# Hybrid decoder layer in two-part fp32: low-part products last, and the modulation matrices one slot later in SP's queue

## The chip, the core and the metric

The kernel runs on one core of one Trainium2 chip. The engines of the core are PE (TensorE, with PEld for its weight loads), DVE (VectorE), ACT (ScalarE), POOL (GpSimd) and SP (SyncE, which here issues all the transfers). The metric is the device time of one execution in microseconds. The time of the kernel before is the median of three runs.

## What is computed

One decoder layer on 512 tokens with model width 1024, then a final RMSNorm. Cut to what matters:

```python
mod = silu(c) @ w_ada + b_ada                        # 6 x 1024 columns
sh1, sc1, gt1, sh2, sc2, gt2 = split(mod, 6)
h = rms_norm(x, g_norm_mix) * (1 + sc1) + sh1
hq, hf, hi, hg, aq, ak, av, ga, gb = split(h @ w_in)  # 8704 columns
y_a = hgrn2_mix(hq, hf, hi, hg, lower_bounds)        # gated linear recurrence, 4 heads
y_b = dilated_mixture(aq, ak, av)                    # 3 groups of 4 heads
merged = sigmoid(ga) * (y_a @ w_branch_a) + sigmoid(gb) * (y_b @ w_branch_b)
x = x + (1 + gt1) * (merged @ w_out)
h2 = rms_norm(x, g_norm_ffn) * (1 + sc2) + sh2
u_gate, u_val = split(h2 @ w_up)
x = x + (1 + gt2) * ((gelu(causal_dwconv(u_gate)) * u_val) @ w_down)
return rms_norm(x, g_final)
```

## The kernel before

**Two-part products.** Every large product is made of three passes. A weight tile and an activation tile are each split into a high part (rounded to fp32r) and a low part (the rest). For each slice k of 128 rows PE multiplies high by high, high weights by low activations, and low weights by high activations, all into one PSUM bank (`three_passes`, products recorded at line L934). A product of 128 x 512 elements is the usual one.

**Units.** The weights come in 75 units of 1 MB. Units 0 to 33 are 256 columns of `w_in`, 34 and 35 are `w_branch_a`, 36 and 37 `w_branch_b`, 38 to 41 `w_out`, 42 to 63 `w_up`, 64 to 74 `w_down`. For each unit:

- SP loads it into `w_raw` (`load_unit`, L465), after it has waited at L463 until the unit two before has both its high and its low part, since it shares the buffer;
- ACT copies it to `w_hi` (L659, `unit_high`), when it has landed and PE has finished the last tile of the unit two before;
- POOL subtracts to give `w_lo` (L590, four instructions, `low_part`);
- PE does `products(u)`: it waits for the low part (`lo_done`), then fills two output tiles (48 products), or four: of 256 columns in units 4, 5, 8, 11, 38 to 41, and over four slices k only in units 34 to 37. A tile takes one of the three banks 0 to 2 in turn. `claim` waits until the bank's tile before has been read out, `filled` tells ACT and DVE that the tile is there. Before the change a tile gets all its products and then the next tile starts.

**Slots.** All engines run the same loop `for u in range(U_UP)`. PE does `products(u)` and then `small(u)`: the small products of the recurrence and the attention, which are laid out over the slots. DVE and ACT do `small_results(u)` and then `evacuate(u)`, each in its own order.

**Modulation.** The modulation matrices 0 to 7 are dealt with at the start. Matrices 8 to 23 (1 MB each, `w_ada`, two buffers `ada2`) are spread over slots 17 to 27 by `MOD_UNITS`: one in slots 17, 18, 21, 24, 25 and 27, two in slots 19, 20, 22, 23 and 26. In slot u DVE scales and adds the matrix (`partial_sums`, L1284 to L1291, the result in `part2`, counted by `part_done`), before it reads out the tiles of unit u. PE ends `small(u)` with eight (or four) products of one column on these sums, after it has waited for `part_done`. SP issues the transfer (L506) when the buffer is free, that is when DVE has summed the matrix two before. SP is strictly in order, so whatever stands behind that wait goes out later.

**Units 36 and 37.** For each of the four tiles DVE multiplies (L1604) and adds (L1606), ACT rounds to `m_hi` (L864), and DVE subtracts to `m_lo` (L1608), before it turns to the next tile. ACT's copy of the high part of unit 38 stands behind the fourth `m_hi` of unit 36.

Of the kernel before, what the change touches and what calls it, by code (L numbers as in the profile page):

```python
# [29 lines left out]
P = 128  # L30
D = 1024
S = 512
KT = D // P
TT = S // P
HEADS = 4
# [21 lines left out]
U_A = U_GB + 4  # L57
U_B = U_A + 2
U_OUT = U_B + 2
# [21 lines left out]
MOD_SLOT, MOD_TWICE = 17, (19, 20, 22, 23, 26)  # L81
MOD_UNITS = {}
# [63 lines left out]
def tiles_of(u):  # L146

    if U_PAIR <= u < U_HG:
        p, what = divmod(u - U_PAIR, 3)
        return 4 if what == 2 and pair(p)[2] == 1 else 2  # L150
    if U_HI <= u < U_PAIR or U_A <= u < U_UP:
        return 4
    return 2
# [41 lines left out]
BANKS = plan_banks()  # L195
# [17 lines left out]
def layer_kernel(nc, x, c, w_ada, b_ada, g_norm_mix, w_in, lb_logits, g_hg_norm, w_branch_a, w_branch_b, w_out,  # L213
                 g_norm_ffn, w_up, conv_w, conv_b, w_down, g_final, out):
    with ExitStack() as ctx:
# [7 lines left out]
        whi = [at(f"w_hi{i}", 136 + 8 * i, [P, 2048], F32R) for i in range(2)]  # L223
        wlo = [at(f"w_lo{i}", 152 + 8 * i, [P, 2048], F32R) for i in range(2)]
# [4 lines left out]
        h_hi = at("h_hi", 168, [P, KT, S], F32R)  # L229
        h_lo = at("h_lo", 184, [P, KT, S], F32R)  # L230
# [24 lines left out]
        ya_hi = at("ya_hi", 40, [P, HEADS, S], F32R)  # L255
        ya_lo = at("ya_lo", 48, [P, HEADS, S], F32R)
# [12 lines left out]
        yb_hi = at("yb_hi", 64, [P, HEADS, S], F32R)  # L269
        yb_lo = at("yb_lo", 76, [P, HEADS, S], F32R)  # L270
# [67 lines left out]
        bank = [ctx.enter_context(nc.psum_tensor(f"bank{i}", [P, 512], F32)) for i in range(8)]  # L338
# [8 lines left out]
        hi_done = sem("hi_done")  # L347
        share_in = [sem(f"share_in{j}") for j in range(KT // 2)]
        hi_share, lo_share = sem("hi_share"), sem("lo_share")
        lo_done = sem("lo_done")  # L350
# [36 lines left out]
        ybfull_done, ybhi_done, yblo_done = sem("ybfull_done"), sem("ybhi_done"), sem("yblo_done")  # L387
# [9 lines left out]
        def claim(eng, name):  # L397

            b, n = BANKS[name]
            if n:  # L400
                eng.wait_ge(free[b], n)
            return bank[b]

        def filled(ins, name):
            ins.then_inc(full[BANKS[name][0]], 1)
# [50 lines left out]
        def _(sp):  # L456
# [34 lines left out]
            for u in range(U_UP):  # L491
                if u == U_B + 2:

                    ready(sp, ("g", U_B - 1, 3))
                    sp.wait_ge(yblo_done, HEADS)
                    sp.dma_start(x1[:, :, :], x_tok).then_inc(x_again, 16)

                    sp.dma_start(gf_row[:, :], g_final.rearrange("(a d) -> a d", a=1).broadcast_to([P, D])).then_inc(gf_in, 16)
                if u >= 3:
                    load_unit(u, unit_source(u), u % 2)  # L500
                if u == MOD_SLOT:
                    ready(sp, ("o", HEADS - 1))
                for n in MOD_UNITS.get(u, ()):
                    if n >= MOD_FIRST + 2:
                        sp.wait_ge(part_done, n - 1)
                    sp.dma_start(ada2[n % 2][:, :, :], cols_of(w_ada, 256 * n)).then_inc(ada2_in[n % 2], 16)  # L506
# [425 lines left out]
        def _(pe):  # L932
            def mm(o, lhsT, rhs, start=True, stop=True, **kw):
                return pe.matmul(o, lhsT, rhs, start=start, stop=stop, **kw)  # L934
# [30 lines left out]
            def unit_parts(u, slot, width):  # L965
                pe.wait_ge(lo_done, u + 1)
                return [w[slot][:, :].rearrange("p (k c) -> p k c", c=width) for w in (whi, wlo)]
# [22 lines left out]
            def plain_tokens(t):  # L990
                return lambda a: a[:, t * P:(t + 1) * P]

            def products(u):
                hT = (h_hi, h_lo)
                n = tiles_of(u)
                width = 512 if U_A <= u < U_OUT else 256
                parts = unit_parts(u, 2 if u == 2 else u % 2, width)
                for t in range(n):
                    b = claim(pe, ("g", u, t))
                    if u == U_A and t == 0:  # L1000
                        pe.wait_ge(yalo_done, HEADS)
                    if u == U_B and t == 0:
                        pe.wait_ge(yblo_done, HEADS)
                    if u >= U_OUT:
                        merged = (m_hi, m_lo)
                        if u == U_OUT and t == 0:

                            token_tile(b[:, 0:256], parts, merged, plain_tokens(0), range(KT - 1))
                            b1 = claim(pe, ("g", u, 1))
                            token_tile(b1[:, 0:256], parts, merged, plain_tokens(1), range(KT - 1))  # L1010
                        kts = range(KT - 1, KT) if u == U_OUT and t < 2 else range(KT)
                        ins = token_tile(b[:, 0:256], parts, merged, plain_tokens(t), kts)
                    elif u >= U_A:
                        ins = feature_tile(b[:, :], parts, t * P, (ya_hi, ya_lo) if u < U_B else (yb_hi, yb_lo), HEADS)
                    elif n == 4:
                        ins = token_tile(b[:, 0:256], parts, hT, plain_tokens(t))
                    else:
                        ins = feature_tile(b[:, :], parts, t * P, hT)
                    filled(ins, ("g", u, t))
# [696 lines left out]
```

## Time and profile before

| | |
|---|---|
| three runs | 1008.28, 1010.56, 1012.77 us; median 1010.56 |
| profiled execution, its own time | 1011.39 us |
| its span | 1009.7 us |
| mean granted clock of TensorE | 0.982 |
| PE busy | 954.7 us, 95% of the span, 4911 products |
| PEld busy | 812.8 us, 80% |
| DVE, POOL, ACT busy | 466.9, 463.4, 367.9 us |

The profiled time is 1.69 us more than its span: that much lies outside the first and the last instruction. A product of PE is recorded with its latency, and the next starts before it has ended, so one reads a stage of PE from start to start: 48 products in 11.03 us, for instance. The granted clock is 1.00 at 2.4 GHz and 0.50 at 1.2 GHz; a stretch in between is a mixture in time of the two.

### The profile page before, as it was taken

How to read it: one execution, taken by the hardware profiler on the slowest of the kernel's cores; microseconds unless marked ns; L12 is line 12 of the kernel's file. 1: busy time of each engine (PE TensorE's matmuls, PEld its weight loads, DVE VectorE, ACT ScalarE, POOL GpSimd, SP SyncE). 2: the span in 40 equal slices, each digit the busy share in tenths (PEclk: the TensorE clock that was granted, in tenths of full speed). 3: DMA queues.
4: the chain of work that ended last, by engine and by line, in shares of the span. 5: the costliest groups of instructions: out<-in, count | busy, mean ns of one | idle time of the engine just before them, and what ended most of it. 6: DMA issues, size and time to landing. Idle time of an engine off the chain costs nothing.

```text
span 1009.7 us, 12653 instructions
## 1 busy us (share of the span) xinstructions
PE 954.7 (95%) x4911; PEld 812.8 (80%) x4911; DVE 466.9 (46%) x720; ACT 367.9 (36%) x499; POOL 463.4 (46%) x382
## 2 busy tenths in 40 slices
PE   2699999999999989899999999899999999999995
PEld 2578989998888878788778899688888888888884
DVE  5855366665337858886642554622222322200006
ACT  6443332424234141444222334544435544412113
POOL 3669542534123243534455455553543453453544
PEclk9989999999999989999999999999999999999998
DMA  9722222121151756362222533123223223223212
GB/s 322 223 83 84 84 84 84 43 84 43 43 167 43 242 175 217 117 209 84 83 84 84 188 101 109 42 83 122 86 83 125 83 83 109 100 87 122 84 42 83
DMA packets 94817, 111.33 MB, mean 110 GB/s; under 512 B 1930, under 2 KB 88118, under 8 KB 94774
## 3 DMA queue, kind: packets, MB, share of 16 engines
q1 hardware_dynamic: 94774, 110.72, 33.3%
q8 instruction: 31, 0.51, 0.2%
q14 instruction: 12, 0.10, 0.0%
HBM read 108.62 MB, written 2.10 MB: 110 GB/s over the span
## 4 chain that ended last, share of the span: by engine, by line
PE 43%; issue 31%; POOL 18%; DVE 5%; ACT 1%; DMA 1%; SPq 0%; POOLq 0%; ACTq 0%; DVEq 0%
PE bank L934 43%; POOL w_lo L590 17%; DVE x L1686 1%; DVE part L1284 1%; DMA x_in<-in_x_dram 1%; DVE h_lo L1301 1%; DVE gelu L1685 0%; DVE part L1295 0%; DVE ada L1284 0%; DVE part L1286 0%; DVE ada L1286 0%; ACT w_hi L659 0%; DVE part L1291 0%; POOL rstd L551 0%; ACT xn_in L703 0%
## 5 line engine op out<-in xcount | busy, mean ns | idle before, releaser
L590 POOL TENSOR_TENSOR w_lo<-w_raw,w_hi 128x512 fp32r<-128x512 f32 x292 | 395.8, 1386 | 494.1 <-ACT w_hi L659 494.1
L934 PE MATMUL bank<-h_hi,w_hi 128*128 128x512 f32 x832 | 332.8, 400 | 9.1 <-POOL w_lo L590 6.0
L934 PE MATMUL bank<-h_hi,w_lo 128*128 128x512 f32 x832 | 329.1, 396 | 0.0
L934 PE MATMUL bank<-h_lo,w_hi 128*128 128x512 f32 x832 | 328.7, 395 | 0.0
L659 ACT ACTIVATE w_hi<-w_raw 128x2048 fp32r<-128x2048 f32 x73 | 139.4, 1909 | 238.1 <-PE bank L934 180.8
L934 PEld LDWEIGHTS bank<-h_hi,w_hi 128*128 128x128 f32 x832 | 159.8, 192 | 44.4 <-POOL w_lo L590 6.2
L934 PEld LDWEIGHTS bank<-h_hi,w_lo 128*128 128x128 f32 x832 | 159.0, 191 | 33.9
L934 PEld LDWEIGHTS bank<-h_lo,w_hi 128*128 128x128 f32 x832 | 159.7, 192 | 32.9
L934 PE MATMUL bank<-w_lo,act_hi 128*128 128x512 f32 x176 | 68.5, 389 | 0.0
L934 PE MATMUL bank<-w_hi,act_lo 128*128 128x512 f32 x176 | 68.5, 389 | 0.0
L934 PE MATMUL bank<-w_hi,act_hi 128*128 128x512 f32 x176 | 68.5, 389 | 0.0
L1660 DVE SCALAR_TENSOR_TENSOR conv<-bank,convc,conv 128x511 f32<-128x511 f32 x22 | 16.4, 745 | 107.8 <-ACT conv L898 107.8
L1685 DVE TENSOR_TENSOR gelu<-bank,g_row 128x512 f32<-128x512 f32 x8 | 5.5, 682 | 107.9 <-PE bank L934 107.9
L1284 DVE SCALAR_TENSOR_TENSOR part<-ada,csilu,part 128x256 f32<-128x256 f32 x64 | 43.8, 685 | 0.0
L1670 DVE TENSOR_TENSOR gelu<-gelu,bank 128x512 f32<-128x512 f32 x22 | 15.1, 687 | 58.3 <-PE bank L934 45.2
L898 ACT ACT_TABLE_LOAD x11 | 14.1, 1283 | 73.8 <-PE bank L934 73.8
L934 PEld LDWEIGHTS bank<-w_hi,act_hi 128*128 128x128 f32 x176 | 33.0, 188 | 6.9
L934 PEld LDWEIGHTS bank<-w_hi,act_lo 128*128 128x128 f32 x176 | 33.0, 188 | 6.9
L934 PEld LDWEIGHTS bank<-w_lo,act_hi 128*128 128x128 f32 x176 | 33.0, 188 | 6.7
L1284 DVE SCALAR_TENSOR_TENSOR ada<-ada,csilu 128x256 f32<-128x256 f32 x56 | 37.4, 669 | 0.0
L934 PE MATMUL bank<-w_hi,m_hi 128*128 128x256 f32 x128 | 36.3, 284 | 0.3 <-POOL w_lo L590 0.3
L934 PE MATMUL bank<-w_hi,h_hi 128*128 128x256 f32 x128 | 36.5, 285 | 0.0
(247 smaller groups left out, 1329.2 us busy)
## 6 DMA issues: line engine op xcount, KB each, us to landing
w_raw<-in_w_in_dram SPq DMA_DIRECT2D x32, 1024.0 KB, 5.2
ada<-in_w_ada_dram SPq DMA_DIRECT2D x24, 1024.0 KB, 7.2
w_raw<-in_w_up_dram SPq DMA_DIRECT2D x22, 1024.0 KB, 5.1
w_raw<-in_w_down_dram SPq DMA_DIRECT2D x11, 1024.0 KB, 4.8
w_raw<-in_w_out_dram SPq DMA_DIRECT2D x4, 1024.0 KB, 6.5
x_in<-in_x_dram SPq DMA_DIRECT2D x4, 512.0 KB, 7.1
w_raw<-in_w_in_dram SPq DMA_DIRECT2D x8, 256.0 KB, 8.5
w_raw<-in_w_branch_a_dram SPq DMA_DIRECT2D x2, 1024.0 KB, 4.9
```

Of the source, the lines that this page charges most:

```text
L590: ins = pool.tensor_tensor(wlo[slot][:, cols], raw[slot][:, cols], whi[slot][:, cols].bitcast(F32), ALU.subtract)
L659: act.activation(whi[bufs][:, :], raw[bufs][:, :], ACT.Copy).then_inc(hi_done, 1)
L898: act.activation(conv[:, t, :], bank[t][:, :], ACT.Identity, scale=CW[:, bass.ds(2 * i + (2 * FT + t), 1)], bias=CW[:, bass.ds(2 * i + (3 ...
L934: return pe.matmul(o, lhsT, rhs, start=start, stop=stop, **kw)
L1284: ins = stt(dst, unit[:, k, :], sc, dst, ALU.mult, ALU.add)
L1301: tt(h_lo[:, k, :], h_part(which, k), h_hi[:, k, :].bitcast(F32), ALU.subtract).then_inc(h_lo_done[k % 2], 1)
L1660: stt(tt_, bank[t][:, 0:S - 1], CW[:, bass.ds(2 * i + (FT + t), 1)], tt_, ALU.mult, ALU.add).then_inc(tap_done, 1)
L1670: tt(gelu[:, t, :], gelu[:, t, :], bank[bk][:, :], ALU.mult).then_inc(free[bk], 1)
L1685: link(tt(gelu[:, half, :], b[:, :], g2_row[:, cols], ALU.mult))
L1686: tt(x1[:, t, cols], x1[:, t, cols], gelu[:, half, :], ALU.add).then_inc(x2_done, 1)
```

## The change

First, PE. For the units 2 to 37 the first two output tiles are now made together: tile 0 gets all its products with the high part of the weights, then tile 1 gets all of its own, then PE waits for the low part, and then both get the products with it. Before the first of them PE waits only for the high part (`hi_done`). Tiles 2 and 3, where a unit has them, are made as before. The number and the form of the products are the same. The bank of tile 1 is claimed 8 products earlier than before (4 in units 34 to 37), and tile 0 is finished 16 products later (8 in units 34 to 37). Second, SP. The modulation matrices of slot u are issued behind the weights of unit u+1, where they stood behind those of unit u.

```diff
@@ SP's queue
                 if u >= 3:
                     load_unit(u, unit_source(u), u % 2)
-                if u == MOD_SLOT:
+                if u - 1 == MOD_SLOT:
                     ready(sp, ("o", HEADS - 1))
-                for n in MOD_UNITS.get(u, ()):
+                for n in MOD_UNITS.get(u - 1, ()):
                     if n >= MOD_FIRST + 2:
                         sp.wait_ge(part_done, n - 1)
                     sp.dma_start(ada2[n % 2][:, :, :], cols_of(w_ada, 256 * n)).then_inc(ada2_in[n % 2], 16)
@@ PE
+            def first_two_tiles(u, width):
...
+                pe.wait_ge(hi_done, u + 1)
+                if u == U_A:
+                    pe.wait_ge(yalo_done, HEADS)
+                if u == U_B:
+                    pe.wait_ge(yblo_done, HEADS)
...
+                for t in range(2):
+                    claim(pe, ("g", u, t))
+                    for k in range(kts):
+                        one_pass(t, k, hi, a_hi, k == 0, False)
+                        one_pass(t, k, hi, a_lo, False, False)
+                pe.wait_ge(lo_done, u + 1)
+                for t in range(2):
+                    for k in range(kts):
+                        ins = one_pass(t, k, lo, a_hi, False, k == kts - 1)
+                    filled(ins, ("g", u, t))
+
             def products(u):
...
+                if u < U_OUT:
+                    first_two_tiles(u, width)
+                    if n == 2:
+                        return
                 parts = unit_parts(u, 2 if u == 2 else u % 2, width)
                 for t in range(n):
+                    if u < U_OUT and t < 2:
+                        continue
                     b = claim(pe, ("g", u, t))
-                    if u == U_A and t == 0:
-                        pe.wait_ge(yalo_done, HEADS)
-                    if u == U_B and t == 0:
-                        pe.wait_ge(yblo_done, HEADS)
```

PE in unit 36 before the change, where tile 0 (bank2) ends and tile 1 (bank0) begins. `yb_hi` and `yb_lo` are the parts of the activations, `w_hi0` and `w_lo0` those of the weights.

```order
L934 MATMUL bank2<-yb_hi_102,w_hi0_51 128x512
L934 MATMUL bank2<-yb_lo_103,w_hi0_51 128x512
L934 MATMUL bank2<-yb_hi_102,w_lo0_53 128x512
L934 MATMUL bank0<-yb_hi_102,w_hi0_51 128x512
L934 MATMUL bank0<-yb_lo_103,w_hi0_51 128x512
L934 MATMUL bank0<-yb_hi_102,w_lo0_53 128x512
```

PE in unit 36 after the change, from the end of tile 1's high products to the start of tile 2 (bank1).

```order
L934 MATMUL bank0<-yb_hi_102,w_hi0_51 128x512
L934 MATMUL bank0<-yb_lo_103,w_hi0_51 128x512
L934 MATMUL bank2<-yb_hi_102,w_lo0_53 128x512 x4
L934 MATMUL bank0<-yb_hi_102,w_lo0_53 128x512 x4
L934 MATMUL bank1<-yb_hi_102,w_hi0_51 128x512
L934 MATMUL bank1<-yb_lo_103,w_hi0_51 128x512
L934 MATMUL bank1<-yb_hi_102,w_lo0_53 128x512
```

Tile 0 was finished as the 12th product of the unit, before tile 1 began; now it is finished as the 20th, and tile 1 as the 24th, as before.

SP's queue before the change, from the weights of unit 19 to those of unit 21 (L465 the weights, L506 the modulation matrices).

```order
L465 DMA w_raw1_50<-in_w_in_dram 128x8x256
L506 DMA ada2_0_123<-in_w_ada_dram 128x8x256
L506 DMA ada2_1_124<-in_w_ada_dram 128x8x256
L465 DMA w_raw0_49<-in_w_in_dram 128x8x256
L506 DMA ada2_0_123<-in_w_ada_dram 128x8x256
L506 DMA ada2_1_124<-in_w_ada_dram 128x8x256
L465 DMA w_raw1_50<-in_w_in_dram 128x8x256
```

SP's queue after the change, again from the weights of unit 19 to those of unit 21.

```order
L465 DMA w_raw1_50<-in_w_in_dram 128x8x256
L506 DMA ada2_1_124<-in_w_ada_dram 128x8x256
L465 DMA w_raw0_49<-in_w_in_dram 128x8x256
L506 DMA ada2_0_123<-in_w_ada_dram 128x8x256
L506 DMA ada2_1_124<-in_w_ada_dram 128x8x256
L465 DMA w_raw1_50<-in_w_in_dram 128x8x256
```

The weights of unit 21 stood behind matrices 12 and 13 of slot 20; now they stand behind matrices 10 and 11 of slot 19 and ahead of those two.

## Rows read from the trace of the kernel before

**Rows 1.** The page: issues of the modulation matrices, their size, median us to landing.

```profile
ada<-in_w_ada_dram SPq DMA_DIRECT2D x24, 1024.0 KB, 7.2
```

**Rows 2.** Waits of PE: total us, times, longest us.

```profile
PE bank L934 <- POOL w_lo L590: 6.3, 4, 3.1
PE bank L934 <- DVE wg_lo L1529: 1.6, 1, 1.6
```

**Rows 3.** Stretches: length; busy (count) of PE, PEld, DVE, ACT, POOL; clock; DMA; GB/s.

```profile
344.13:355.16 11.03, 11.03 (x51) 9.10 (x50) 8.87 (x22) 1.15 (x1) 0.00 (x0) 1.00 1.01 322
361.02:374.56 13.54, 13.54 (x48) 10.89 (x49) 7.90 (x11) 4.42 (x18) 5.61 (x4) 0.80 0.33 109
406.72:419.34 12.62, 12.62 (x49) 10.24 (x50) 9.88 (x17) 5.74 (x19) 5.11 (x4) 0.86 0.47 154
486.08:498.71 12.63, 12.63 (x50) 10.02 (x49) 4.87 (x5) 1.23 (x2) 5.19 (x4) 0.87 0.24 83
641.50:860.00 218.50, 218.50 (x965) 180.91 (x965) 59.63 (x86) 102.98 (x104) 99.22 (x80) 1.00 0.29 96
```

**Rows 4.** Timeline (start, us, ...) of PE at the starts of units 21, 23, 24.

```profile
356.94 0.95 PE L934 MATMUL bank<-ones,part 128*128 128x1 f32 x8
361.02 0.79 PE L934 MATMUL bank<-h_hi,w_hi 128*128 128x512 f32 x1 [3.13 <-POOL w_lo L590]
...
389.48 1.00 PE L934 MATMUL bank<-ones,part 128*128 128x1 f32 x8
390.34 0.48 PE L934 MATMUL bank<-h_hi,w_hi 128*128 128x512 f32 x1
...
403.11 0.95 PE L934 MATMUL bank<-ones,part 128*128 128x1 f32 x8
406.72 0.50 PE L934 MATMUL bank<-h_hi,w_hi 128*128 128x512 f32 x1 [2.65 <-POOL w_lo L590]
```

**Rows 5.** Timeline of SP: matrices 12 and 13, weights of unit 21, matrices 15 and 16.

```profile
336.12 7.77 SPq L506 DMA_DIRECT2D ada<-in_w_ada_dram  x2
344.01 0.51 SPq L465 DMA_DIRECT2D w_raw<-in_w_in_dram  x1
...
354.40 15.06 SPq L506 DMA_DIRECT2D ada<-in_w_ada_dram  x2
```

**Rows 6.** Timeline of ACT and POOL: the two parts of unit 21's weights.

```profile
354.01 1.92 ACT L659 ACTIVATE w_hi<-w_raw 128x2048 fp32r<-128x2048 f32 x1 [15.96 <-DMA w_raw<-in_w_in_dram]
...
356.01 4.96 POOL L590 TENSOR_TENSOR w_lo<-w_raw,w_hi 128x512 fp32r<-128x512 f32 x4 [12.79 <-ACT w_hi L659]
```

**Rows 7.** Timeline of DVE: matrices 13 and 15 begin, 16 ends, then unit 22's tiles.

```profile
350.85 0.35 DVE L1286 TENSOR_SCALAR part<-ada,csilu 128x256 f32<-128x256 f32 x1 [1.76 <-DMA ada<-in_w_ada_dram]
...
378.73 0.34 DVE L1286 TENSOR_SCALAR part<-ada,csilu 128x256 f32<-128x256 f32 x1
...
389.39 0.43 DVE L1291 TENSOR_TENSOR part<-part,ada 128x256 f32<-128x256 f32 x1
389.73 1.28 DVE L1566 COPY ka<-bank 128x512 f32<-128x512 f32 x2
```

**Rows 8.** Timeline of DVE in units 36 and 37, without most of its rows.

```profile
563.08 0.69 DVE L1604 TENSOR_TENSOR sgb<-sgb,bank 128x512 f32<-128x512 f32 x1 [2.94 <-PE bank L934]
...
566.16 0.68 DVE L1604 TENSOR_TENSOR sgb<-sgb,bank 128x512 f32<-128x512 f32 x1
...
569.26 0.68 DVE L1604 TENSOR_TENSOR sgb<-sgb,bank 128x512 f32<-128x512 f32 x1
...
571.97 0.68 DVE L1604 TENSOR_TENSOR sgb<-sgb,bank 128x512 f32<-128x512 f32 x1
```

**Rows 9.** Timeline of ACT, POOL and PE: the weights of unit 38 and its start.

```profile
573.94 1.90 ACT L659 ACTIVATE w_hi<-w_raw 128x2048 fp32r<-128x2048 f32 x1
...
575.92 6.41 POOL L590 TENSOR_TENSOR w_lo<-w_raw,w_hi 128x512 fp32r<-128x512 f32 x4 [8.53 <-ACT w_hi L659]
...
582.39 0.38 PE L934 MATMUL bank<-w_hi,m_hi 128*128 128x256 f32 x1 [0.31 <-POOL w_lo L590]
```

More of the change, by code:

```diff
@@ L991, in plain_tokens, with one_pass @@
                 return lambda a: a[:, t * P:(t + 1) * P]
+            def first_two_tiles(u, width):
+                slot = 2 if u == 2 else u % 2
+                hi, lo = (w[slot][:, :].rearrange("p (k c) -> p k c", c=width) for w in (whi, wlo))
+                tokens_out = tiles_of(u) == 4 and u < U_A
+                a_hi, a_lo = (h_hi, h_lo) if u < U_A else (ya_hi, ya_lo) if u < U_B else (yb_hi, yb_lo)
+                kts = KT if u < U_A else HEADS
+                pe.wait_ge(hi_done, u + 1)
[3 more added lines that the diff above has]
+                    pe.wait_ge(yblo_done, HEADS)
+                def one_pass(t, k, w, a, start, stop):
+                    tile, o = slice(t * P, (t + 1) * P), bank[BANKS["g", u, t][0]]
+                    if tokens_out:
+                        return mm(o[:, 0:256], a[:, k, tile], w[:, k, :], start, stop, skip_group_check=True)
+                    return mm(o[:, :], w[:, k, tile], a[:, k, :], start, stop, skip_group_check=True)
+                for t in range(2):
[8 more added lines that the diff above has]
+                    filled(ins, ("g", u, t))
             def products(u):
```

## The prediction, made before the changed kernel ran

> **What bounds the kernel now.** PE is busy in 95% of the span of 1009.7 us, so the question is only where PE stands still and where its clock is low. I read first the waits of PE. In the part that the change touches (units 2 to 37) two releasers matter: the low part of the weights, 6.3 us in four waits of which the longest is 3.1, and once the DVE chain that makes the merge weights, 1.6 us [rows 2]. The timeline puts 3.13 and 2.65 us of them at the starts of units 21 and 24 [rows 4] and 0.31 us at unit 38 [rows 9]; the 0.2 us left of the 6.3 stand at unit 27. Then I read stretches for the clock. A unit of 48 products takes 11.03 us at clock 1.00, that is 0.230 us for a product; unit 21 took 13.54 us at 0.80, unit 24 took 12.62 us at 0.86, and unit 30, right behind the wait for the merge weights, 12.63 us at 0.87 [rows 3]. Each slow unit is one that begins after PE stood still: after 3.13, 2.65 and 1.57 us [rows 2, 4]. Behind the 0.31 us of unit 38 the clock stayed.
>
> Last I followed the low part of unit 21 back. POOL made it from 356.01 to 360.97, ACT the high part from 354.01 to 355.93, and ACT had waited 15.96 us for the transfer [rows 6]. SP issued that transfer at 344.01, right behind two modulation matrices, of which the second went out only at 336.12 + 7.77 = 343.89, when DVE had freed its buffer [rows 5]. So the stall is one of SP's order: weights queue behind a modulation matrix that queues behind DVE. Unit 24 is the same case.
>
> **The change part by part.**
>
> *The number of products* does not change, nor their form, so PE's own work costs nothing more. The order of the banks changes from product to product at most as it does in the loop of the gate projections, which alternates two banks after every three products and ran at clock 1.00 over 218.50 us with 965 recorded products, 0.226 us each [rows 3].
>
> *The waits for the low part.* After eight one-column products PE needs 0.86 us to the first product of the next unit where nothing holds it (389.48 to 390.34) [rows 4]. So unit 21 could have begun at 356.94 + 0.86 = 357.80 and began at 361.02: 3.22 us. Unit 24: 403.97 against 406.72, 2.75 us. Unit 27: the 0.2 us left above. Sum 6.17 us. Either half of the change takes them away alone. With the split, unit 21 needs only the high part, there at 355.93, before 357.80; the low part is needed 32 products later, 32 x 0.230 = 7.4 us, and it was there 3.2 us after 357.80. With SP's new order the weights of unit 21 stand behind matrices 10 and 11, whose place in DVE is a slot earlier; they go out before the pair that now stands at 336.12 to 343.89 [rows 5], at least 7.9 us earlier than at 344.01, so the high part too is there before 357.80 with time to spare, and the low part, 7.0 us behind its start (354.01 to 360.97), by 353.1. What is late next at these starts is nothing: PE itself.
>
> *The clock.* Unit 21 took 13.54 - 11.03 = 2.51 us more than a unit at full clock, unit 24 took 12.62 - 11.03 = 1.59 us more [rows 3]. The idle time that stood before both is gone, so I count both: 4.10 us.
>
> *The modulation matrices one slot later.* Each is issued when both the weights ahead of it are out and DVE has summed the matrix two before. The first condition is new by one unit. In the trace the second is the later one except for matrices 15 and 20, one each behind the low part of a unit that came late. Matrix 15 was issued at 354.40 [rows 5] and would now wait for the low part of unit 21, which ended at 360.97 when its weights were late [rows 6]. Even then, with 7.2 us for the transfer [rows 1], it would have landed at 368.2, and DVE came to it at 378.73 [rows 7]. Cost 0. The second matrix of a double slot lands as late as now: DVE waited 1.76 us for matrix 13 [rows 7], and a load of weights followed it at once (343.89 and 344.01 [rows 5]), as one does in the new order.
>
> *DVE and PE at the end of the double slots.* These are tight. The sum of matrix 16 ends at 389.82, PE's one-column products on it began at 389.48 and took 1.00 instead of 0.95 us [rows 4, 7]. DVE starts its slot when PE ends the one before, so the pair moves together and the stall does not grow. Bound: 0 to 0.5 us in each of slots 19, 22, 26; I take 0, as the row shows it.
>
> *Tile 0 later, bank of tile 1 earlier.* In a unit of 48 products tile 0 is there 16 x 0.230 = 3.7 us later, and PE wants its bank again at the 16th product of the next unit. The latest reading is in unit 22: DVE frees tile 0 halfway through 389.73 to 391.01, at about 390.4 [rows 7]; PE claims that bank 16 products into unit 23, at 390.34 + 3.7 = 394.0 [rows 4]. Margin 3.6 us. It costs nothing there or elsewhere in this stage, but 3.6 us is all the cover there is.
>
> *Units 36 and 37* have no such cover. There DVE and ACT take as long for a tile as PE: 3.08 us for the first (563.08 to 566.16, while POOL works), 2.71 us for the third (569.26 to 571.97) [rows 8], against 12 x 0.230 = 2.76 us of PE. DVE was idle for 2.94 us ahead of the first tile, waiting for PE. That tile now comes 8 x 0.230 = 1.84 us later, and nothing behind it can catch up except the 3.08 - 2.71 = 0.37 us that the first step may win if POOL's work lies less on it. So the fourth `m_hi`, and ACT's copy of unit 38's weights behind it at 573.94, come 1.47 to 1.84 us later, and so does POOL's low part, 575.92 to 582.33, for which PE already waits 0.31 us [rows 9]. Unit 38 is not split. Loss 1.5 to 1.8 us; I take 1.6. The idle time becomes 0.31 + 1.6 = 1.9 us. Behind 1.57 us of idle time the clock fell in unit 30, where some small products stood between, and it cost 12.63 - 11.03 = 1.60 us [rows 3]; behind 0.31 it did not. Bounds 0 and 1.6 us; I take 0 and keep the other end for the range.
>
> Here the Trainium skill has a rule on the cause of the 3.08 us: "SBUF — State Buffer", section "SBUF: two separate sides", says that a DVE operation with two SBUF inputs and a GpSimd operation shut each other out of a port pair. By it the 0.37 us comes back only if POOL's low part of unit 37 ends before DVE's first addition, so the loss would be the upper end, 1.8 us.
>
> *The wait for the merge weights*, 1.57 us [rows 2], ends a DVE chain that starts when PE ends slot 27, so it moves with PE and stays, and its lost clock with it.
>
> **Sum.** 6.17 + 4.10 - 1.6 = 8.67 us. On the profiled execution's own time 1011.39 - 8.67 = 1002.7. That execution lay 0.83 us over the median of the runs, 1010.56, so as a median 1002.7 - 0.8 = **1001.9 us**.
>
> **The rivals.**
>
> *The cover in DVE is too thin (a wait takes the place of the one removed).* With PE no longer stalled, DVE and ACT have no slack from it. For it: the 0.05 us at 389.48 above. Price: 1 us in each of slots 19, 22 and 26, and one low-clock unit of 1.6 us: 4.6 us given back, 1001.9 + 4.6 = 1006.5. Nearly the same time comes if the idle time goes and the clock is lost elsewhere all the same: 1001.9 + 4.1 = 1006.0.
>
> *The loss at unit 38 doesn't come*, because the chain of DVE and ACT catches up in unit 36: 1001.9 - 1.6 = 1000.3; if unit 30 keeps its clock as well, another 1.6 less, 998.7.
>
> *Slower.* SP now waits for unit u+1's buffer (L463) before it may issue the matrices of slot u. If POOL's low part of unit u-1 ended later than DVE's sum of the matrix two before, and by more than the matrix lies in wait, DVE would stand for the transfer, PE behind its sums, and POOL behind PE. It decides from the point where the issue comes less than 7.2 us [rows 1] before DVE's use. In three double slots this is 3 x 7.2 = 21.6 us and, as in unit 21, 2.5 us of clock each: 29.1 us, which makes 1001.9 + 29.1 = 1031.0. Against it speaks the margin of matrix 15, 378.7 - 368.2 = 10.5 us.
>
> *Banks in turn.* Between two passes PE goes back to a bank that it left. The gate projections do so oftener, at clock 1.00 [rows 3]; were the clock lost for 1.6 us in each of the 36 units, the time would be 1001.9 + 57.6 = 1059.5. The Trainium skill, "TensorE: Matmul & The Clock Gate", section "A second HAM failure mode: psum-queue depth-cycling", reports a kernel in which cycling through banks made TensorE idle briefly and its clock swing. This case's 218.50 us at clock 1.00 does not agree with it.
>
> *The change does nothing* if something other than the weights holds PE at these starts: 1010.6.
>
> **Chances.** Forecast (1000.3 to 1003.6) 0.61; thin cover or clock lost elsewhere (1003.6 to 1007) 0.19; no loss at unit 38 (998.5 to 1000.3) 0.11; nothing 0.04; slower 0.04; banks 0.01. About 0.5%, 5 us, is what a measurement of this kernel can tell from no change; the bound lies at 1005.5. Of the second case I put a third below it. Faster by over 0.5%: 0.61 + 0.11 + 0.06 = 0.78. Within: 0.13 + 0.04 = 0.17. Slower: 0.05. Range for 8 in 10: down to 999.0, and up to 1006.5 for most of the second case, with the 1.6 us of clock at unit 38 inside it.
>
> **What would show it.** Right: no idle time of PE at the starts of units 21 and 24, both at about 11.1 us; the transfer of unit 21's weights issued before 336 us on the old scale; the wait of PE at unit 38 near 1.9 us, with `m_hi` and ACT's copy of unit 38 late by the same; the wait for the merge weights as before. Wrong: waits of PE on DVE's `part` or on a bank's release in slots 18 to 28, a DVE wait for `ada` much over 1.76 us, or units 36 and 37 ending without a longer wait behind them.

## The result, and the profile after

The changed kernel takes **1004.07 us** (median of 8 runs, 1002.87 to 1007.33) where the kernel before, on the same chip, took 1010.35 us (8 runs, 1006.61 to 1013.98). The ratio is 0.9946, 95% interval 0.9925 to 0.9968: about 0.5% faster. The medians lie 6.3 us apart; the ratio is estimated from all runs, here and below, and isn't the quotient of the two medians. The profiled execution took 1005.12 us with a span of 1003.4 us, against 1011.39 and 1009.7 before. The forecast was 1001.9, its range 999.0 to 1006.5.

The waits of PE (total us, times, longest us), after:

```profile
PE bank L934 <- POOL w_lo L590: 2.1, 1, 2.1
PE bank L934 <- DVE wg_lo L1561: 1.6, 1, 1.6
...
PE bank L934 <- DVE part L1323: 0.8, 1, 0.8
```

The four waits for `w_lo`, 6.3 us in all [rows 2], are now one of 2.1 us. The wait for the merge weights, `wg_lo`, stayed at 1.6. A wait for `part` is new in this profile.

The timeline of PE at the starts of units 21 and 24, after (start, us, ...):

```profile
357.69 0.49 PE L934 MATMUL bank<-h_hi,w_hi 128*128 128x512 f32 x1
...
398.07 0.49 PE L934 MATMUL bank<-h_hi,w_hi 128*128 128x512 f32 x1
```

Neither start has a wait in brackets any more, against 3.13 and 2.65 us [rows 4]. Unit 21 starts 3.33 us earlier than before, unit 24 8.65 us earlier.

SP's timeline around the weights of unit 21 (line 465) and the matrices (line 506), after:

```profile
327.34 0.37 SPq L506 DMA_DIRECT2D ada<-in_w_ada_dram  x1
327.81 0.53 SPq L465 DMA_DIRECT2D w_raw<-in_w_in_dram  x1
```

The weights of unit 21 went out at 327.81; before the change they went out at 344.01, behind a matrix that had to wait for its buffer [rows 5].

Stretches, after (length; busy and count of PE, PEld, DVE, ACT, POOL; clock; DMA; GB/s):

```profile
357.69:368.72 11.03, 11.03 (x51) 9.05 (x50) 7.67 (x22) 3.91 (x17) 4.64 (x4) 1.00 0.58 183
398.07:409.10 11.03, 11.03 (x51) 9.05 (x50) 8.62 (x24) 5.19 (x18) 4.63 (x4) 1.00 0.88 279
475.35:482.18 6.83, 6.83 (x17) 4.91 (x16) 5.40 (x6) 0.91 (x2) 5.91 (x4) 0.50 0.07 25
477.17:490.60 13.43, 13.43 (x50) 10.64 (x49) 4.02 (x4) 1.23 (x2) 4.45 (x3) 0.81 0.24 78
```

Units 21 and 24 take 11.03 us each at clock 1.00, against 13.54 at 0.80 and 12.62 at 0.86 [rows 3]. Unit 30 got worse: 13.43 us at 0.81 against 12.63 at 0.87 [rows 3]. The 0.50 in the third row is the lower level, 1.2 GHz, and it lasts 6.83 us.

The end of slot 26, after: timelines of POOL, DVE and PE.

```profile
427.08 5.46 POOL L590 TENSOR_TENSOR w_lo<-w_raw,w_hi 128x512 fp32r<-128x512 f32 x4 [7.86 <-ACT w_hi L659]
...
431.31 1.51 DVE L1316 SCALAR_TENSOR_TENSOR part<-ada,csilu,part 128x256 f32<-128x256 f32 x1
432.74 0.47 DVE L1316 SCALAR_TENSOR_TENSOR ada<-ada,csilu 128x256 f32<-128x256 f32 x1
...
437.54 0.43 DVE L1323 TENSOR_TENSOR part<-part,ada 128x256 f32<-128x256 f32 x1
...
438.02 0.61 PE L934 MATMUL bank<-ones,part 128*128 128x1 f32 x4 [0.81 <-DVE part L1323]
438.49 0.48 PE L934 MATMUL bank<-h_hi,w_hi 128*128 128x512 f32 x1
```

As long as POOL works on the low part of unit 27, DVE's multiply-add takes 1.51 us, and after that 0.47. Four of DVE's operations are stretched in this way (three multiply-adds, and the scaling before them from 0.35 to 1.46 us), about 4 us in all, and the sum of the second matrix ends at 437.97, when PE already waits for it. In the kernel before, POOL made this low part from 442.14, over the last three operations of the chain, and PE lost only the 0.20 us for `w_lo`:

```profile
442.56 1.51 DVE L1284 SCALAR_TENSOR_TENSOR part<-ada,csilu,part 128x256 f32<-128x256 f32 x1
...
442.14 5.89 POOL L590 TENSOR_TENSOR w_lo<-w_raw,w_hi 128x512 fp32r<-128x512 f32 x4 [12.69 <-ACT w_hi L659]
...
448.09 0.51 PE L934 MATMUL bank<-h_hi,w_hi 128*128 128x512 f32 x1 [0.20 <-POOL w_lo L590]
```

Last, the start of unit 38, after: timelines of DVE (first tile of unit 36), ACT, POOL and PE.

```profile
556.78 0.69 DVE L1636 TENSOR_TENSOR sgb<-sgb,bank 128x512 f32<-128x512 f32 x1 [4.75 <-PE bank L934]
557.50 1.42 DVE L1638 TENSOR_TENSOR sgb<-sgb,sga 128x512 f32<-128x512 f32 x1
...
567.15 0.63 ACT L864 ACTIVATE m_hi<-sgb 128x512 fp32r<-128x512 f32 x1 [2.08 <-DVE sgb L1638]
567.69 1.90 ACT L659 ACTIVATE w_hi<-w_raw 128x2048 fp32r<-128x2048 f32 x1
...
569.67 6.38 POOL L590 TENSOR_TENSOR w_lo<-w_raw,w_hi 128x512 fp32r<-128x512 f32 x4 [11.30 <-ACT w_hi L659]
...
576.10 0.39 PE L934 MATMUL bank<-w_hi,m_hi 128*128 128x256 f32 x1 [2.13 <-POOL w_lo L590]
```

DVE waits 4.75 us for the first tile instead of 2.94 [rows 8], and PE waits 2.13 us at unit 38 instead of 0.31 [rows 9]: 1.81 and 1.82 us more.

**The account of the span**, by start times (before minus after, rows above and [rows 3, 4, 9]):

| point | before | after | earlier by | step |
|---|---|---|---|---|
| unit 21 starts | 361.02 | 357.69 | 3.33 | |
| unit 24 ends | 419.34 | 409.10 | 10.24 | |
| unit 27 starts | 448.09 | 438.49 | 9.60 | -0.64 |
| unit 30 starts | 486.08 | 477.17 | 8.91 | -0.69 |
| unit 30 ends | 498.71 | 490.60 | 8.11 | -0.80 |
| unit 38 starts | 582.39 | 576.10 | 6.29 | -1.82 |
| span ends | 1009.7 | 1003.4 | 6.3 | 0 |

### The profile page after: what moved, and what is told of

Same layout as the page of the kernel before. It is cut to its first block, busy times and chain, and to the rows that moved or that the text cites. A ratio compares the mean times of both kernels' runs of the same rounds, so it can differ in the third digit from the quotient of the medians.

```text
span 1003.4 us, 12661 instructions
## 1 busy us (share of the span) xinstructions
PE 950.4 (95%) x4911; PEld 809.4 (81%) x4911; DVE 465.7 (46%) x720; ACT 368.3 (37%) x499; POOL 460.5 (46%) x382
## 4 chain that ended last, share of the span: by engine, by line
PE 43%; issue 30%; POOL 18%; DVE 5%; ACT 1%; DMA 1%; SPq 0%; POOLq 0%; ACTq 0%; DVEq 0%
PE bank L934 43%; POOL w_lo L590 17%; DVE x L1718 1%; DVE part L1316 1%; DMA x_in<-in_x_dram 1%; DVE h_lo L1333 1%; DVE gelu L1717 0%; DVE part L1327 0%; DVE ada L1316 0%; DVE part L1318 0%; DVE ada L1318 0%; ACT w_hi L659 0%; DVE part L1323 0%; POOL rstd L551 0%; ACT xn_in L703 0%
## 5 line engine op out<-in xcount | busy, mean ns | idle before, releaser
L934 PE MATMUL bank<-h_hi,w_lo 128*128 128x512 f32 x832 | 257.8, 392 | 0.0
L934 PE MATMUL bank<-w_lo,m_hi 128*128 128x256 f32 x128 | 36.2, 283 | 0.0
L934 PE MATMUL bank<-w_hi,m_lo 128*128 128x256 f32 x128 | 36.2, 283 | 0.0
```

## The experiments

The theory to test: SP's order alone removes the stalls; the split has nothing left to cover after it, and in units 36 and 37 it costs 1.8 us. Its rivals: the split carries part of the gain, or the loss at unit 38 has another cause. Three groups of kernels ran, each with the kernel before beside it. Medians are compared only within a group, ratios also between groups. Medians in us, ratio to before:

| kernel | before | median (range) | ratio, 95% |
|---|---|---|---|
| SP's order alone | 1006.72 | 1001.55 (998.42 to 1004.63) | 0.9947, 0.9921 to 0.9972 |
| split alone | 1006.72 | 1004.11 (1001.20 to 1006.36) | 0.9970, 0.9945 to 0.9995 |
| whole, 36 and 37 not split | 1006.72 | 1001.77 (998.46 to 1003.62) | 0.9951, 0.9923 to 0.9979 |
| before, unit 36 alone split | 1006.72 | 1011.60 (1003.25 to 1016.12) | 1.0038, 1.0007 to 1.0070 |
| whole change again | 1008.46 | 1004.10 (1001.60 to 1006.73) | 0.9961, 0.9943 to 0.9978 |
| whole, ACT copies early | 1008.46 | 1003.05 (1002.22 to 1005.12) | 0.9947, 0.9926 to 0.9968 |
| whole, merge weights later | 1008.46 | 1000.75 (999.75 to 1002.02) | 0.9923, 0.9899 to 0.9946 |
| SP's order, early copies, merge later | 1008.46 | 1000.83 (997.78 to 1001.50) | 0.9915, 0.9893 to 0.9937 |
| whole, `m_lo` one tile late | 1008.12 | 1001.25 (999.65 to 1005.49) | 0.9950, 0.9927 to 0.9973 |
| SP's order, merge later, `m_lo` late | 1008.12 | 997.96 (996.49 to 998.43) | 0.9905, 0.9878 to 0.9932 |
| whole, merge later, `m_lo` late | 1008.12 | 999.16 (998.07 to 1000.79) | 0.9919, 0.9892 to 0.9946 |
| kernel before again | 1008.12 | 1008.86 (1006.20 to 1011.21) | 1.0022, 0.9998 to 1.0045 |

### The whole change again

> The whole change once more, beside the others. My theory: as before, 0.9946 of the kernel before, PE waiting 2.1 us at unit 38. With the half of SP alone at 0.9947 and the half of PE alone at 0.997, it should not be faster than SP's half: about 1.8 us slower than that (1003 where SP's half gave 1001.6). Rival (the halves add up): 2.6 us faster than SP's half alone.

The ratio, 0.9961, overlaps the first one, and the gains of the two halves don't add up. This profile differs from the first at two places. Two stretches, unit 30 and unit 38:

```profile
476.55:487.64 11.09, 11.09 (x50) 8.93 (x49) 4.96 (x5) 1.23 (x2) 5.28 (x4) 1.00 0.29 95
...
573.14:586.25 13.11, 13.11 (x96) 13.11 (x97) 6.82 (x11) 4.60 (x9) 5.42 (x4) 0.87 0.30 90
```

Unit 30 kept its clock behind the same wait of 1.6 us, and unit 38 lost it behind its 2.1 us. In the first profile it was the other way round: unit 30 took 13.43 us at 0.81, and unit 38 ran at clock 1.00. So what a wait of this size costs in clock is not fixed by the program.

### SP's order alone

```
-                if u == MOD_SLOT:
+                if u - 1 == MOD_SLOT:
...
-                for n in MOD_UNITS.get(u, ()):
+                for n in MOD_UNITS.get(u - 1, ()):
```

> Only SP's new order, PE as before the change. My theory: the stalls at units 21 and 24 come from the order in SP's queue alone, so this half alone takes away 3.2 and 2.8 us of idle time and 4.1 us of low clock, as the whole change does, and it has not the loss of 1.8 us at unit 38, which is the split's: about 1.8 us faster than the whole change, 1002.3 as a median against 1004.1. PE at unit 38 waits 0.3 us as before. Rival (the split is what saves the starts): stalls stay, over 1008.

One of PE's waits, and the start of unit 38:

```profile
PE bank L934 <- DVE part L1291: 0.8, 1, 0.8
...
572.43 0.38 PE L934 MATMUL bank<-w_hi,m_hi 128*128 128x256 f32 x1 [0.31 <-POOL w_lo L590]
```

No stall is left at units 21, 24 and 27, unit 38 waits only 0.31 us, and the median is 5.2 us under that of before. The wait for `part` in slot 26 comes without any split: the weights of unit 27 are there earlier, so POOL starts earlier and stretches more of DVE's sums. The 1.8 us by which this kernel should beat the whole change show in the traces, as the missing loss at unit 38, but not in the times: the ratios are 0.9947 here and 0.9946 and 0.9961 for the whole change.

### The split alone

`first_two_tiles` for all units below `U_OUT`, SP's loop as before.

> Only PE's split, SP's order as before the change. My theory: the high part of unit 21 is there at 355.9, before PE wants it, so the starts of units 21 and 24 are as short as in the whole change, with the full clock, and unit 38 waits 2.1 us: about the time of the whole change, 1004.1. Rival (PE then waits in the middle of units 21 and 24 for the low part, or DVE's late reading of tile 0 shows): waits of 1 us and more inside these units, 1006 to 1009.

The start of unit 21 on PE, its low part on POOL, the start of unit 38 on PE:

```profile
356.12 0.49 PE L934 MATMUL bank<-h_hi,w_hi 128*128 128x512 f32 x1
...
352.15 5.00 POOL L590 TENSOR_TENSOR w_lo<-w_raw,w_hi 128x512 fp32r<-128x512 f32 x4 [10.17 <-ACT w_hi L659]
...
572.78 0.39 PE L934 MATMUL bank<-w_hi,m_hi 128*128 128x256 f32 x1 [2.13 <-POOL w_lo L590]
```

The split does what it says: PE starts at 356.12, though the low part is ready only at 352.15 + 5.00 = 357.15, and the unit runs through. But unit 38 again waits 2.13 us, now without SP's new order. This half alone gains 2.6 us in the median, half of the 5.2 us of SP's order; the 1.8 us at unit 38 are the larger part of the difference.

### The whole change, with units 36 and 37 left as they were

```
-                if u < U_OUT:
+                split = u < U_B
+                if split:
                     first_two_tiles(u, width)
```

> The whole change, but units 36 and 37 made tile by tile as before the change. My theory: the loss at unit 38 goes, PE waits 0.3 us there instead of 2.1, and the time is 1.8 us below that of the whole change, 1002.3. Rival (unit 38 is late because of SP's order or of the shift in time): the wait of 2.1 us stays, 1004.1.

```profile
574.39 0.39 PE L934 MATMUL bank<-w_hi,m_hi 128*128 128x256 f32 x1 [0.31 <-POOL w_lo L590]
```

PE's timeline at unit 38: the wait is back at 0.31 us. The median, 1001.77, is that of SP's order alone, 1001.55. The other 34 split units add nothing to SP's order that can be measured.

### The kernel before, with unit 36 alone split

`split = u == U_B`, SP's loop as before.

> The kernel before with the split in unit 36 alone. My theory: the first tile of unit 36 comes 1.8 us later, the chain of DVE and ACT can't catch up, ACT's copy of unit 38's weights and POOL's low part come 1.8 us later, and PE's wait at unit 38 grows from 0.3 to 2.1 us; stretches ahead of unit 36 as before; 1.8 us slower than before, 1012.2 against 1010.35. Rival: no change.

Start and stretch of unit 38:

```profile
583.67 0.39 PE L934 MATMUL bank<-w_hi,m_hi 128*128 128x256 f32 x1 [2.13 <-POOL w_lo L590]
...
583.67:596.77 13.10, 13.10 (x96) 13.10 (x97) 6.82 (x11) 4.60 (x9) 5.42 (x4) 0.87 0.29 91
```

One split unit suffices for the whole 2.13 us, so it is the late first tile of unit 36 that costs, as the prediction had it. In this profile the clock fell too: the 96 products took 13.10 us at 0.87, where the first profile of the whole change shows 11.61 at 1.00. The kernel is slower than before, 1.0038 with an interval above 1. The medians differ by 4.9 us, more than the 1.8 expected; the interval of the ratio, 0.7 to 7.0 us, includes the 1.8 and doesn't tell what the rest is.

### The whole change, ACT copying the high parts of units 38 and 39 ahead of `m_hi`

```
+                        if t == 3:
+                            unit_high(u + 2)
...
-                if u >= 2:
+                if u >= 2 and u not in (U_B + 1, U_B + 2):
                     unit_high(u + 1)
```

> The whole change, and ACT copies the high parts of units 38 and 39 ahead of the fourth m_hi of units 36 and 37 instead of behind it. My theory: the loss at unit 38 comes through ACT's order only, so POOL's low part of unit 38 is there before PE needs it, PE's wait falls from 2.1 us to below 0.5, and the time is 1.8 us below the whole change. Rival (PE then waits for m_lo, since DVE's chain is late by the same 1.8 us): the wait moves into unit 38, with m_lo as its releaser, and over 1 us of the 1.8 stays.

ACT, then PE in unit 38:

```profile
562.11 1.92 ACT L659 ACTIVATE w_hi<-w_raw 128x2048 fp32r<-128x2048 f32 x1
...
570.71 0.28 PE L936 MATMUL bank<-w_hi,m_hi 128*128 128x256 f32 x1
...
575.21 0.38 PE L936 MATMUL bank<-w_hi,m_hi 128*128 128x256 f32 x1 [2.09 <-DVE m_lo L1642]
```

ACT's copy of unit 38's weights is the first row. Unit 38 starts without a wait, and PE then waits 2.09 us inside it for `m_lo`. The wait has moved, not gone, as the rival said. The median is 1.05 us below that of the whole change in the same group, 1003.05 against 1004.10, which these runs can't tell from no change. The weights are one of two things that come late by the same time; the chain of DVE and ACT over the tiles, at 2.7 us a tile, is the other.

### The whole change, merge weights used one slot later

`SLOT_BC = SLOT_STAT + 4` instead of `+ 3`.

> The whole change, and the products that spread the merge weights (bc) stand one slot later, in slots 30 to 33. My theory: the wait of 1.6 us for the merge weights goes, and with it the low clock in unit 30 (0.8 to 2.5 us by its place): 2.4 to 4 us faster than the whole change. Rival (clock falls there for the small products, not for the wait): 1.6 us faster, and unit 30 or 31 still over 12 us.

```profile
473.46:484.43 10.97, 10.97 (x49) 8.82 (x47) 1.69 (x1) 3.00 (x3) 5.03 (x4) 1.00 0.45 144
```

The stretch is unit 30: 10.97 us at clock 1.00, and the wait for `wg_lo` is gone. The median falls by 3.35 us against the whole change in the same group, within the 2.4 to 4 expected. 1.6 us of it are the wait. That the rest is clock is a reading and not shown: the two profiles of the whole change lost about 3 and 0 us of clock behind that wait.

### SP's order, early copies and later merge weights, no split

> SP's half alone, with the early copy for units 38 and 39 and the merge products a slot later. My theory: no split, so no loss at unit 38, and the 0.3 us there and the stall for the merge weights gone: 2.5 to 4 us below SP's half alone (1001.6), so 998 to 999, the fastest of these.

The stretch of unit 38, and its first product behind the wait in it:

```profile
568.65:583.75 15.10, 13.24 (x97) 13.03 (x96) 8.31 (x14) 5.22 (x10) 5.49 (x4) 0.89 0.41 138
...
572.82 0.39 PE L936 MATMUL bank<-w_hi,m_hi 128*128 128x256 f32 x1 [1.86 <-DVE m_lo L1610]
```

Here unit 38 had only 0.31 us to lose, and the early copy brought in 1.86 us of wait and a lower clock: the copy of 1.92 us stands ahead of an `m_hi` for which DVE and PE wait. The copy was in its right place. The expected 998 to 999 us, the fastest of these, was missed: the median is 1000.83, that of the whole change with later merge weights alone (1000.75), and the error was to take the early copy for free.

### The whole change, `m_lo` one tile later in units 36 and 37

```
-                        dve.wait_ge(mhi_done, f + 1)
-                        tt(m_lo[:, f, :], ...)
+                        for e in {0: (), 1: (f - 1,), 2: (f - 1,), 3: (f - 1, f)}[t]:
+                            dve.wait_ge(mhi_done, e + 1)
+                            tt(m_lo[:, e, :], ...)
```

> The whole change, and VectorE in units 36 and 37 makes the low half of tile f-1 (m_lo) only after the multiply and add of tile f, so that it no longer waits 0.7 us in each tile for ScalarE's m_hi. Theory (the wait in front of unit 38 comes from the chain of VectorE and ScalarE on m_hi and m_lo, 2.7 us a tile, not from the weights' load): the wait of TensorE before unit 38 falls from 2.1 to under 0.5 us, and the kernel is about 1.8 us faster than the whole change, ratio to before near 0.993 to 0.994. Rival (the late start of the chain by the doubled pair 36/37 alone sets it, and the 0.7 us are slack): the wait stays at 2 us or goes inside unit 38 as a wait for m_lo, and the time is that of the whole change, 0.995 to 0.996.

Waits of PE, DVE at the first tile of unit 37 (multiplication, then addition), POOL at unit 38's low part:

```profile
PE bank L934 <- DVE m_lo L1641: 1.3, 1, 1.3
...
568.82 0.69 DVE L1636 TENSOR_TENSOR sgb<-sgb,bank 128x512 f32<-128x512 f32 x1 [1.73 <-PE bank L934]
569.54 1.80 DVE L1638 TENSOR_TENSOR sgb<-sgb,sga 128x512 f32<-128x512 f32 x1
...
568.25 5.95 POOL L590 TENSOR_TENSOR w_lo<-w_raw,w_hi 128x512 fp32r<-128x512 f32 x4 [8.72 <-ACT w_hi L659]
```

The wait for the weights is gone, as the theory said, but 1.3 us come back inside unit 38, as a wait for `m_lo`. The theory's under 0.5 us was wrong, and the rival came nearer: it named such a wait, if a longer one, and the time of the whole change, 0.995 to 0.996, and the ratio is 0.9950. Two things make `m_lo` late in unit 37. DVE now waits 1.73 us for PE at the first tile of that unit, which the split delivers later, and POOL's low part of unit 38 lies over DVE's work, where an addition takes 1.80 instead of 0.69 us. The next two kernels tell which counts: without the split POOL lies over DVE's work on unit 37 as well (one `m_lo` takes 1.78 us there), and PE doesn't wait for `m_lo`; with the split the 1.3 us are back. So the late first tile of unit 37 is what makes PE wait here. No run splits unit 37 alone.

### SP's order, later merge weights and later `m_lo`, with and without the split

> The kernel before with SP's reorder alone, the merge weights' statistics one slot later for their reader (SLOT_BC + 1), and the same delayed m_lo in units 36 and 37; no unit is split. Theory (with the weights early, the split of low products adds nothing; what is left are the merge-weights wait and unit 38): the stalls before units 21 and 24, the one after unit 29 and the one before unit 38 are all gone; 9 to 11 us under before in the trace, ratio 0.990 to 0.992. Rival (the split still gives something, by cover for the low part): this kernel is slower than the one with the split by 0.5 us or more and shows w_lo or w_hi waits at units 21 to 27.

> The whole change, SLOT_BC + 1 and the delayed m_lo in units 36 and 37. Theory: the same time as the kernel with SP's reorder alone and the same two edits, within 0.5 us, since the split has no stall left to cover; the 0.8 us wait for part in slot 26 stays. Rival (the doubled slots couple VectorE and TensorE and cost something in each): slower than it by 1 us or more; or (the split still covers) faster by 0.5 us or more.

Two stretches without the split, units 30 and 38:

```profile
473.22:484.19 10.97, 10.97 (x50) 8.82 (x48) 1.68 (x1) 3.00 (x3) 5.03 (x4) 1.00 0.43 144
569.18:581.02 11.84, 11.76 (x98) 11.56 (x97) 6.31 (x11) 4.44 (x9) 5.42 (x4) 1.00 0.35 111
```

Unit 38 with the split:

```profile
570.21:583.35 13.14, 11.84 (x98) 11.62 (x96) 7.54 (x13) 4.60 (x9) 5.42 (x4) 1.00 0.32 102
```

Without the split this is the fastest kernel of the study, 997.96 us, ratio 0.9905. With it the median is 999.16, 1.2 us more; the ranges of the two meet only at their ends, though the intervals of their ratios overlap. The profile shows where the time goes: unit 38 takes 13.14 us, of which PE is busy 11.84, against 11.84 and 11.76. The rest is a wait of 1.3 us for `m_lo`. The first text expected stalls gone and 0.990 to 0.992, and got both; the second expected the same time within 0.5 us, and its rival, 1 us or more by coupling, came true, though at units 36 to 38 and not in the double slots: the 0.8 us of `part` are in both.

### The kernel before, once more

> The kernel before once more, for another profiled execution. Theory (the loss before units 21 and 24 is a race of the weights' transfers, started late, against TensorE, and so varies from run to run): the waits before units 21 and 24 come again, at the same units, of 2 to 4 us each, sizes other than in the first profile by some tenths, and stretches at the lower granted clock behind them of 0, 3.4 or 6.8 us. Rival (they are fixed by the program): both waits and both low stretches repeat within 0.1 us. Ratio 1.000 within 0.003.

PE at the starts of units 21 and 24, SP and ACT for unit 21's weights, the stretches of units 21 and 24, and one of PE's waits:

```profile
360.00 0.50 PE L934 MATMUL bank<-h_hi,w_hi 128*128 128x512 f32 x1 [1.16 <-POOL w_lo L590]
...
403.08 0.50 PE L934 MATMUL bank<-h_hi,w_hi 128*128 128x512 f32 x1 [0.95 <-POOL w_lo L590]
...
343.96 0.51 SPq L465 DMA_DIRECT2D w_raw<-in_w_in_dram  x1
...
352.97 1.92 ACT L659 ACTIVATE w_hi<-w_raw 128x2048 fp32r<-128x2048 f32 x1 [13.84 <-DMA w_raw<-in_w_in_dram]
...
360.00:372.63 12.63, 12.63 (x48) 10.21 (x49) 8.85 (x17) 4.71 (x18) 5.05 (x4) 0.86 0.21 66
403.08:414.10 11.02, 11.02 (x48) 9.06 (x49) 10.74 (x20) 6.89 (x19) 5.13 (x4) 1.00 0.40 129
...
PE bank L934 <- DVE part L1291: 0.6, 1, 0.6
```

The waits come at the same two units but are 1.16 and 0.95 us, not 3.13 and 2.65 [rows 4], so the 2 to 4 us expected of each were wrong, and the theory that they vary holds more strongly than it was put. The weights of unit 21 went out at the same time (343.96 and 344.01), landed 1.04 us sooner (352.97 and 354.01 [rows 6]), and PE came to the unit 0.95 us later (360.00 - 1.16 against 361.02 - 3.13 [rows 4]). Unit 24 kept its clock. And the wait for `part` is there too, 0.6 us: with less of a stall ahead, POOL comes to the low part of unit 27 earlier in the slot in this kernel as well. The two stalls and their clock cost here 1.16 + 0.95 + (12.63 - 11.03) = 3.7 us, in the first profile 3.13 + 2.65 + (13.54 - 11.03) + (12.62 - 11.03) = 9.9 us.

There is a third view of the same two stalls. The kernel with unit 36 alone split is the kernel before up to that unit. PE at the starts of units 21 and 24 there:

```profile
360.41 0.79 PE L934 MATMUL bank<-h_hi,w_hi 128*128 128x512 f32 x1 [2.44 <-POOL w_lo L590]
...
406.15 0.50 PE L934 MATMUL bank<-h_hi,w_hi 128*128 128x512 f32 x1 [2.61 <-POOL w_lo L590]
```

Its unit 21 took 13.64 us at clock 0.79 and its unit 24 12.62 us at 0.86, so the two stalls cost 2.44 + 2.61 + 2.61 + 1.59 = 9.25 us, nearly what they cost in the first profile.

## Why the prediction was right, and where it was off

**Right: the stalls and their clock.** The steps for units 21 and 24 gave 3.22 + 2.75 + 4.10 = 10.07 us; at the end of unit 24 the two profiles are 10.24 us apart. The chain behind it (weights behind a matrix behind DVE) is shown by SP's order alone, which removes both stalls, and by the split alone, which does so in another way. "Either half of the change takes them away alone" was right. The stalls vary, but not so much that chance could explain this: all ten profiles with SP's new order are without them, three of these without the split, and all three profiles with the old order and no split in units 21 and 24 show both. As said there, matrices a slot later cost no further wait for `ada` (4.4 us in all after the change, 5.0 before), and changing the bank between passes cost nothing: units 21 and 24 ran at clock 1.00 in 11.03 us each.

**Right: the loss at unit 38.** Predicted 1.5 to 1.8, taken 1.6; measured 1.82 in the wait. The upper end was the true one: DVE's first tile came 1.81 us late and nothing of it was caught up. The prediction let only the first step of DVE win time, but the second was long as well (566.16 to 569.26 is 3.10 us [rows 8]). After the change the second step took 2.71 us and won 0.39, and the first took 3.51 us and lost 0.43, because POOL still worked on the low part of unit 37 when DVE's first addition began (1.42 us). The sentence on the Trainium skill, "SBUF — State Buffer", section "SBUF: two separate sides", gave this end, and the trace agrees with it. That unit 36 alone brings the whole wait, and that it is gone when 36 and 37 stay as they were, shows the cause. The forecast's 0 for clock held in the first profile; in two of the five profiles with the 2.13 us wait the clock fell.

**Off: the double slots.** The bound of 0 to 0.5 us, taken as 0, failed in slot 26: the wait for `part` was 0.81 us, and the start of unit 27 had lost 0.64 us against the end of unit 24, where the prediction had 0.2 us more of gain. The step that failed is "the pair moves together". It left out that earlier weights let POOL work earlier, over DVE's sums, whose operations then take 1.5 instead of 0.5 us. A wait for `part` in slots 18 to 28 was one of the signs of being wrong that the prediction had named. The same section of the Trainium skill, "SBUF — State Buffer", "SBUF: two separate sides", has the rule for this too, that a DVE operation with two SBUF inputs and a GpSimd operation lock each other out, and the 1.51 against 0.47 us agree with it; the prediction applied it to units 36 and 37 and not here. Only part of the 0.8 us is the change's, since another profile of the kernel before shows 0.6 us of it. The row that could have told it stood in the trace of before, 442.56 with 1.51 us.

**Off: unit 30.** The prediction said that the wait for the merge weights "stays, and its lost clock with it". The wait did (1.6 us in both profiles), the clock did not. It was low for 6.83 us instead of 3.41, from before the start of the unit, and this took 0.69 + 0.80 = 1.49 us. In the same program's second profile no clock was lost there. Behind the same wait of 1.6 us ten profiles show no low stretch in two, 3.4 us in four (the first of the kernel before among them), 6.8 us in four. This is scatter and not an effect of the change. The term should have been a range, from 0 to the 3 us of this profile: 13.43 - 11.09 in the unit and 0.69 ahead of it.

So in the profile 8.67 became 10.24 - 0.64 - 1.49 - 1.82 = 6.29. This is the rival of the thin cover in DVE, or of clock lost elsewhere, in both its halves, each smaller than priced (0.8 us once, not 1 us three times), and the time, 1004.07, lies in its part of the range.

**Off: one profile taken for the kernel.** The prediction set the profile's sum against the median and moved it by 0.8 us. But the stalls themselves vary: 9.9 and 3.7 us in the two profiles of the kernel before, 9.25 us in the third view of them, and its runs spread from 997.84 to 1011.74 in one group. The gain in the medians was 6.3 us in the first comparison and 4.4 in the second. The mean of the three profiles is 7.6 us, below the 10.07 that the sum took from one; three are few, and the median of the stalls isn't known. Some luck is in how near the forecast came: in the comparison that it is held against, the kernel before had its highest median, 1010.35 us, where the later groups show 1006.72 to 1008.46.

**What the parts are worth.** By the traces, SP's order brings all of the gain. The split covers the same stalls, so it adds nothing to that in units 2 to 35, and costs 1.8 us at unit 38. By the times, SP's order alone and the whole change can't be told apart. I can't say from these runs what the split would give where weights come late for another reason.

## What to carry to other kernels

When a stall comes from weights that queue behind another transfer, move the transfer; reordering products to hide the same stall is a second cure for one illness, and it delivers the first tile later to whoever reads it. Before moving a transfer earlier, ask what the engine that it wakes will run beside: here a subtraction on POOL that came to lie over DVE's multiply-adds, with two SBUF inputs each, made them three times as long. Price a stall that is a race of a transfer against PE from more than one profile.

## What the runs showed that was not expected

- DVE's multiply-add on 128x256 takes 0.47 to 0.50 us alone and 1.51 us while POOL's subtraction runs; the effect starts and ends with POOL's work, to within one operation. An addition on 128x512 in unit 37 went from 0.69 to 1.80 us. A multiplication with one input in a PSUM bank (L1636) stayed at 0.68 us beside POOL. POOL's own four operations took 5.46 and 5.89 us beside DVE's sums of slot 26, up to 6.41 us in units 36 and 37 [rows 9], and 4.96 us for unit 21 [rows 6].
- The granted clock behind an idle time of 1.6 to 2.1 us falls in some executions and not in others of the same program: unit 30 of the whole change took 13.43 us in one profile and 11.09 in the other, unit 38 kept clock 1.00 in the first and ran at 0.87 in the second.
- A stretch at the lower clock can cost next to nothing. In the kernel before, the first products of the FFN ran at 0.50. After the change they ran at 1.00, and PE then waited 1.28 us for DVE's `h_lo` a second time; the two profiles are 6.29 us apart at the start of unit 38 and 6.3 at the end of the span, so the full clock won nothing in between. The first row is of before, the second of after:

```profile
636.06:639.48 3.42, 2.80 (x7) 2.26 (x8) 3.42 (x4) 0.52 (x1) 3.42 (x3) 0.50 0.02 5
```

```profile
634.94 0.51 PE L934 MATMUL bank<-h_hi,w_hi 128*128 128x512 f32 x1 [1.28 <-DVE h_lo L1333]
```
